# A hybrid attention and convolution backbone on one core: the sink logit as a score column, and rows of h that all start 160 bytes past a multiple of 256

## The reference

```python
h = modulate(rmsnorm(x, g_mix[l]), sh1, sc1)
hc = modulate(rmsnorm(ctx, g_mix[l]), csh1, csc1)
q, k, v, u = split_in(h @ w_in[l])
...
s_loc = jnp.einsum('bnqhgd,bnkhd->bnhgqk', qb, kb).astype(jnp.float32) * SCALE
s_loc = jnp.where(valid[None, :, None, None], s_loc, NEG_INF)
s_ctx = jnp.einsum('bnqhgd,bchd->bnhgqc', qb, k_ctx).astype(jnp.float32) * SCALE
s_sink = jnp.broadcast_to(sink.astype(jnp.float32).reshape(N_KV_HEADS, GROUP, 1, 1), ...)
p = jax.nn.softmax(jnp.concatenate([s_loc, s_ctx, s_sink], axis=-1), axis=-1)
...
x = x + gt1 * merge_groups(a_out, cv_out, g_attn_out[l], g_conv_out[l], w_out[l])
h2 = modulate(rmsnorm(x, g_ffn[l]), sh2, sc2)
x = x + gt2 * swiglu(h2, w_gate_up[l], w_down[l])
```

## Time and profile before

| | us |
|---|---|
| median of 3 runs | 1558.81 (1558.37 to 1560.59) |
| the profiled execution | 1558.88 |
| its span | 1557.1 |
| layer 0: first products of h to the end of attention | 42 to 307 |
| layer 0: output projection and FFN | 308 to 945 |
| layer 1: products of h up to the attention | 945 to 1060 |
| layer 1: attention | 1060 to 1132 |
| layer 1: output projection, FFN, last norm | 1132 to 1557 |

### The profile page before, as it was taken

How to read it: one execution, slowest core, us unless ns; L and a number is a source line. 1 busy time by engine, 2 the same in 40 slices (tenths; PEclk the granted TensorE clock), 3 DMA queues, 4 the chain that set the end, 5 groups by cost and what they waited for, 6 DMA issues and landing times.

```text
span 1557.1 us, 22716 instructions
## 1 busy us (share of the span) xinstructions
PE 1514.7 (97%) x8830; PEld 1227.4 (79%) x8830; DVE 917.5 (59%) x1529; ACT 535.0 (34%) x869; POOL 103.1 (7%) x147
## 2 busy tenths in 40 slices
PE   5999998999999999999999999999999999999997
PEld 2875775588888888888888888776679888888886
DVE  2684679777566425665863366869977533333335
ACT  3311469725322112221112243238835322222232
POOL 0043100040000000000000000530020000000000
PEclk9999999999999999999999999999999999999999
DMA  9582510013333123433431123520012332322222
GB/s 354 222 230 76 205 52 28 1 41 122 108 121 121 54 94 109 148 114 123 168 108 54 57 65 108 142 67 15 28 58 92 95 96 96 104 96 94 95 91 85
DMA packets 39865, 161.16 MB, mean 104 GB/s; under 512 B 5616, under 2 KB 6000, under 8 KB 33648
## 3 DMA queue, kind: packets, MB, share of 16 engines
q1 hardware_dynamic: 35856, 148.72, 27.9%
q0 software_dynamic: 3936, 11.45, 2.7%
HBM read 149.76 MB, written 2.10 MB: 98 GB/s over the span
## 4 chain that ended last, share of the span: by engine, by line
PE 90%; DVE 5%; ACT 2%; issue 2%; DMA 1%; SPq 0%; DVEq 0%; ACTq 0%
PE banks L514 75%; PE banks L543 3%; PE banks L655 2%; PE banks L667 2%; PE banks L682 2%; PE banks L451 2%; PE banks L717 1%; PE banks L483 1%; PE banks L501 1%; ACT prob L882 1%; DVE row_max L1232 1%; ACT probT L894 1%; DMA ada_first<-in_w_ada 1%; DVE ada_sum_context L1199 0%; DVE x L1208 0%
## 5 line engine op out<-in xcount | busy, mean ns | idle before, releaser
L798 ACT ACTIVATE w_high<-raw 128x1024 fp32r<-128x1024 f32 (+2 forms) x182 | 186.2, 1023 | 714.7 <-PE banks L514 701.6
L1113 DVE TENSOR_TENSOR w_low<-raw,w_high 128x1024 fp32r<-128x1024 f32 (+2 forms) x182 | 217.3, 1194 | 228.2 <-ACT w_high L798 224.8
L514 PE MATMUL banks<-h_high,w_high 128*128 128x512 f32 (+1 forms) x1248 | 309.9, 329 | 2.9 <-DVE tmp L1160 1.1
L514 PE MATMUL banks<-h_high,w_low 128*128 128x512 f32 (+1 forms) x1248 | 304.1, 325 | 0.0
L514 PE MATMUL banks<-h_low,w_high 128*128 128x512 f32 (+1 forms) x1248 | 303.2, 324 | 0.0
L514 PEld LDWEIGHTS banks<-h_high,w_high 128*128 128x128 f32 x1248 | 192.7, 188 | 38.0 <-issue 16.9
L514 PEld LDWEIGHTS banks<-h_low,w_high 128*128 128x128 f32 x1248 | 192.9, 188 | 20.9
L514 PEld LDWEIGHTS banks<-h_high,w_low 128*128 128x128 f32 x1248 | 191.5, 188 | 20.5
L1159 DVE COPY shift_product<-banks 128x2 f32<-128x2 f32 x78 | 12.4, 159 | 198.7 <-PE banks L514 188.1
L514 PE MATMUL banks<-h_normal_high,w_high 128*128 128x512 f32 x304 | 118.3, 389 | 0.0
L514 PE MATMUL banks<-h_normal_low,w_high 128*128 128x512 f32 x304 | 118.3, 389 | 0.0
(11 more groups left out here) (195 smaller groups left out, 2173.6 us busy)
## 6 DMA issues: line engine op xcount, KB each, us to landing
raw<-in_w_gu SPq DMA_DIRECT2D x88, 512.0 KB, 3.5
ada_raw<-in_w_ada SPq DMA_DIRECT2D x21, 1024.0 KB, 5.7
raw<-in_w_dn SPq DMA_DIRECT2D x32, 512.0 KB, 3.5
raw<-in_w_mix SPq DMA_DIRECT2D x28, 512.0 KB, 5.0
ada_in_ff<-in_w_ada SPq DMA_DIRECT2D x12, 1024.0 KB, 5.5
raw<-in_w_out SPq DMA_DIRECT2D x16, 512.0 KB, 3.5
ada_first<-in_w_ada SPq DMA_DIRECT2D x7, 1024.0 KB, 14.4
raw<-in_w_dn SPq DMA_DIRECT2D x16, 384.0 KB, 3.0
```

The lines of the kernel that those rows point to most:

```text
L514: last = mm(bank[:, 2 * slot + bk, 0:b - a], weights[w][:, k0_w + k, :], rhs[:, k0_rhs + k, a:b], start=(k == 0 and n == 0), stop=(k == kt ...
L798: last = f(wH[j][:, at, :], raw[j][:, at, :], ACT.Copy)
L1113: last = tt(wL[j][:, at, :], raw[j][:, at, :], f32(wH[j][:, at, :]), ALU.subtract)
```

## The change

- Queries are multiplied by SCALE when they are split into high and low, so the scores come scaled (`q_high`, `q_low`; TENSOR_TENSOR becomes SCALAR_TENSOR_TENSOR there).
- The sinks are split into three bf16 parts once, at the start, in three rows of a zero tensor; `scores` gets one more product, a bf16 tile of ones by a column of that tensor, which writes the sink logit as one more score column.
- `row_max` runs over the scores and that column and writes its result negated; `neg_max` is gone. The exponential covers the column too, so the row sum has the sink in it; `esink` and `add_sink` are gone.
- DVE's order in a step is invert(n+2), divide(n+2), row_max(n+4).
- `h_high` and `h_low` become one tensor with rows of 832 floats (3328 bytes, 13 x 256). The token columns of every row of both start 160 bytes past a multiple of 256, the shift columns for the latents sit directly before them and those for the context directly behind. Where a pass is split 256 and 258, it is now 258 (two shift columns and 256 tokens) and 256.
- The room for software DMA descriptors is 8192 bytes per partition in place of 16384. Every other tensor keeps its place against the 256-byte grid, or is one that the products of L514 don't read.

```diff
-HC = N + 2
-HW = HC + L + 2
+H0 = 64
+HW = H0 + T
+LINE = 8
...
+        sb("gap_line_h", [P, LINE])
-            hH = h_scope.enter_context(nc.sbuf_tensor("h_high", [P, DT, HW], F32R))
-            hL = h_scope.enter_context(nc.sbuf_tensor("h_low", [P, DT, HW], F32R))
+            h_both = h_scope.enter_context(nc.sbuf_tensor("h_both", [P, 2 * DT * HW + H0 + 56], F32R))
+            flatH, flatL = h_both[:, 0:DT * HW + H0], h_both[:, DT * HW:2 * DT * HW + H0]
+            hH, hL = Rows(flatH), Rows(flatL)
...
-            return [(0, 0, N), (1, HC, HW)] if context else [(0, 0, N // 2), (1, N // 2, HC)]
+            if context:
+                return [(0, H0, H0 + N), (1, H0 + N, HW + 2)]
+            return [(0, H0 - 2, H0 + N // 2), (1, H0 + N // 2, H0 + N, 2)]
...
+                    h = g * GRP + i
+                    parts.append((first + P * len(keys), 1, onesb[:], sink_rows[:, layer, h:h + 1]))
...
-                    f(probs[u % 4][:, 0:w], score_place(u, qs[q][2]), ACT.Exp,
-                      bias=nmax[:, c:c + 1], scale=SCALE, accum_out=psums[:, c:c + 1])
-                    f(esink[:, c:c + 1], col("sink", qs[q][0] * GRP + i, layer), ACT.Exp,
-                      bias=nmax[:, c:c + 1]).then_inc(exp_ok, 1)
+                    f(probs[u % 4][:, 0:w + 1], score_place(u, qs[q][2]), ACT.Exp,
+                      bias=nmax[:, c:c + 1], accum_out=psums[:, c:c + 1]).then_inc(exp_ok, 1)
...
-                    nc.vector.reduce_max(mx[:, c:c + 1], score_place(u, qs[q][2]), AX.X).then_inc(row_ok, 1)
...
+                    nc.vector.reduce_max(nmax[:, c:c + 1], score_place(u, qs[q][2]), AX.X, negate=True).then_inc(max_ok, 1)
...
                     if 0 <= n + 2 < len(order):
-                        add_sink(n + 2)
+                        invert(n + 2)
+                        divide(n + 2)
                     if n + 4 < len(order):
                         row_max(n + 4)
-                    if 0 <= n + 2 < len(order):
-                        invert(n + 2)
-                    if n + 4 < len(order):
-                        neg_max(n + 4)
-                    if 0 <= n + 2 < len(order):
-                        divide(n + 2)
...
+            for n in range(3):
+                rest = sink_rest[:] if n else sinks
+                row = slice(32 * n, 32 * n + 1)
+                chain.link(nc.vector.tensor_copy(sink_part[:], rest))
+                made = nc.vector.tensor_copy(sink_rows[row], sink_part[row])
+                if n == 2:
+                    made.then_inc(sinks_ok, 1)
+                else:
+                    chain.link(tt(sink_rest[:], rest, sink_part[:], ALU.subtract))
```

More of the change, by code:

```diff
@@ L113, in queries, with __init__, __getitem__ @@
             for b in range(TB if layer == 0 else NB)]
+class Rows:
+    def __init__(self, flat):
+        self.flat = flat
+    def __getitem__(self, key):
+        _, k, cols = key
+        return self.flat[:, k * HW + cols.start:k * HW + cols.stop]
 class Chain:
@@ L512, in tile_product @@
                     for n, (weights, rhs) in enumerate(((wH, rhsH), (wH, rhsL), (wL, rhsH))):
-                        for bk, a, b in cols:
-                            last = mm(bank[:, 2 * slot + bk, 0:b - a], weights[w][:, k0_w + k, :],
+                        for bk, a, b, *to in cols:
+                            to = to[0] if to else 0
+                            last = mm(bank[:, 2 * slot + bk, to:to + b - a], weights[w][:, k0_w + k, :],
                                       rhs[:, k0_rhs + k, a:b], start=(k == 0 and n == 0),
@@ L636, in scores @@
                         pe.wait_ge(conv_ok, (CT - 1) * (layer + 1))
+                        pe.wait_ge(sinks_ok, 1)
                     if n < 2:
@@ L767, in _ @@
                               (layer, "n2") if c == 0 else None, blocks)
-                    phase(layer, f"dn{c}", tiles, ffH[layer], ffL[layer], tok_cols(context, False),
+                    phase(layer, f"dn{c}", tiles, ffH[layer], ffL[layer], tok_cols(context),
                           (ff_low, layer * FT + sum(CHUNKS[:c])))
@@ L824, in high @@
                 for a, b, scale in scales:
-                    last = f(hH[:, k, hcols(a, b)], src[:, a:b], ACT.Copy, scale=scale)
+                    last = f(tileH[:, k, hcols(a, b)], src[:, a:b], ACT.Copy, scale=scale)
                 last.then_inc(high_ok, 1)
             def shift_high(layer, shift):
-                for at in (N, HW - 2):
-                    last = f(hH[:, :, at:at + 2], mod[:, layer, shift * DT:(shift + 1) * DT, :], ACT.Copy)
+                for to in shiftsH:
+                    last = f(to, mod[:, layer, shift * DT:(shift + 1) * DT, :], ACT.Copy)
                 last.then_inc(sh_high, 1)
@@ L875, in exponential @@
                 def exponential(n):
-                    u, (q, i) = unit0 + n, order[n]
+                    u, (q, _) = unit0 + n, order[n]
                     w, c = P * len(qs[q][2]), u % 4
@@ L1076, in dn_pair @@
                                     for a, b, v in streams(True):
-                                        last = f(hH[:, t, hcols(a, b)], x[:, t, a:b], ACT.Copy,
+                                        last = f(tileH[:, t, hcols(a, b)], x[:, t, a:b], ACT.Copy,
                                                  scale=gain[:, layer + 1, 0, bass.ds(t, 1), v])
@@ L1144, in low @@
                 for a, b, scale in scales:
-                    last = stt(out=hL[:, k, hcols(a, b)], in0=src[:, a:b], scalar=scale,
-                               in1=f32(hH[:, k, hcols(a, b)]), op0=ALU.mult, op1=ALU.subtract)
+                    last = stt(out=tileL[:, k, hcols(a, b)], in0=src[:, a:b], scalar=scale,
+                               in1=f32(tileH[:, k, hcols(a, b)]), op0=ALU.mult, op1=ALU.subtract)
                 last.then_inc(h_ok, 1)
@@ L1150, in shift_low @@
                 dve.wait_ge(sh_high, 2 * layer + (1 if shift == 0 else 2))
-                for at in (N, HW - 2):
-                    last = tt(hL[:, :, at:at + 2], mod[:, layer, shift * DT:(shift + 1) * DT, :],
-                              f32(hH[:, :, at:at + 2]), ALU.subtract)
+                for to, high in zip(shiftsL, shiftsH):
+                    last = tt(to, mod[:, layer, shift * DT:(shift + 1) * DT, :], f32(high), ALU.subtract)
                 last.then_inc(sh_ok, 1)
@@ L1265, in attention @@
                 row_max(0)
-                neg_max(0)
                 rope_product(layer, LAST_Q, context)
```

84 lines of the change are left out of this document (40 added, 44 removed).

## The result

The changed kernel takes 1545.12 us (median of 4 runs, 1544.04 to 1545.38) against 1558.59 us for the kernel before in the same session: a ratio of 0.9911, 95% interval 0.9896 to 0.9925, 13.5 us faster. The prediction said 1553.3 us, 1548.5 to 1559.5. The profiled execution took 1544.04 us with a span of 1542.2.

The account below looks back on a forecast made before the run. PE was taken to bound the kernel, busy 97% of the span and 90% of the chain. Terms -4.5 - 6.3 + 1.3 + 2.9 + 1.0 = -5.6 us from 1558.88 gave 1553.3 us, range 1548.5 to 1559.5.

Parts of the forecast that it names:

- Rows of h: Main products on h in layer 0: 2880 matmuls at 173.95 ns in place of 175.5, 4.5 us gained; layer 1 at 0.
- 0.45 ns a column: Products on h: price per column from a pair of ff, making one more column per matmul 173.5 + 0.45 = 173.95 ns.
- The rival that the placing brings nothing: Products on h: their new starts gain nothing, total gain only 1.1 us, 1557.8 us; chance 0.15.
- The removed instructions: Attention: pieces on the chain of esink (3.8 us), neg_max (2.1) and add_sink (0.4), 6.3 us gained; elsewhere worth nothing.
- The column: Attention on PE: the sink's one-column product costs 0.06 us on 48 units of the chain, 2.9 us (0.5 to 5.8).
- The division behind the inverse: Attention on DVE: division starts 0.20 us after the inverse, 0.13 us back on about ten units, 1.3 us lost.
- What stays: Attention: 1.0 us (0 to 2) of the 6.3 remains because PE's own string or the probabilities' copy is late next.
- Between 236 and 262: Layer 0's attention, where ACT is the chain: units some 2 us shorter in all.
- The column's own rival: Attention on PE: switching weights to the ones and back costs 0.24 us a unit, 11.5 us, giving 1561.9; chance 0.08.
- the late maximum: Attention on DVE: maximum comes too late, 0.4 us in each of 32 units, +12.8 us, giving 1566; chance 0.05.
- More is gained: Whole kernel: column hides at 0.01 us, nothing stays, h reaches ff's pace; -10.3 us, 1548.6; chance 0.12.
- What costs nothing: Query scaling, start-up sink rows, smaller descriptor room (2.1 us slack) and one more column in maximum and exponential: no term.

Follow-up runs that it names:

- rows_32: The changed kernel with all rows of h starting 32 bytes past a multiple of 256 in place of 160; 1554.24 us, ratio 0.9968.
- rows_128: The changed kernel with all rows of h starting 128 bytes past a multiple of 256 in place of 160; 1553.61 us, ratio 0.9966.
- rows_192: The changed kernel with all rows of h starting 192 bytes past a multiple of 256 in place of 160; 1554.89 us, ratio 0.9969.
- rows_only: The kernel before with only the new rows of h and the smaller descriptor room, attention as before; 1553.45 us, ratio 0.9967.
- all_back: The changed kernel with small exponential, sum step and negation put back as idle copies in DVE's old order, sink column kept; 1552.95 us, ratio 0.9964.
- two_columns: The changed kernel with a second one-column product, of zeros, onto the same score column in every unit; 1546.45 us, ratio 0.9921.
- no_column: The changed kernel without the sink's product and its score column, so the softmax leaves out the sink; 1544.13 us, ratio 0.9908.
- max_first: The changed kernel with DVE's order maximum, inverse, division in place of inverse, division, maximum; 1545.60 us, ratio 0.9912.
- att_only: The kernel before with only the change of attention, rows of h and descriptor room as before; 1552.15 us, ratio 0.9956.
- esink_back: The changed kernel with the sink's small exponential on ACT put back behind every exponential, its result unused, only signalling; 1553.02 us, ratio 0.9949.
- add_back: The changed kernel with a small DVE instruction, multiplying the sum by one, put between exponential and inverse; 1548.76 us, ratio 0.9936.
- weights_0: The changed kernel, rows of h at 160, with weight tiles moved from 128 past a multiple of 256 to a multiple; 1562.70 us, ratio 1.0025.

## Why the prediction was wrong

**Rows of h: mechanism right, term too small.** Forecast -4.5 us for 2880 products at 173.95 ns, and 0 for layer 1. Measured 173.4 ns: 2.1 ns less each, 6.0 us by the product, and 6.7 us in all stretches of h together, layer 1's included (its 222 products went from 120.7 to 118.5 ns, where I had counted that one gain and one loss cancel). The step that failed is the added "0.45 ns a column": a pair of h takes the 347 ns of a pair of ff, so the two extra columns are free. The second step is layer 1, put at 0: its stretches gave 1.3 of the 6.7 us. The intervals from start to start show where the gain lies. Before, 231.0 ns follow a product of 512 columns and 119.8 one of 258; after, 230.0 and 116.7. Most came from the context columns, which had started 8 bytes past a multiple of 16. Some of that comes with all the even starts tried: in rows_32, rows_128 and rows_192 the 258 columns take 117.6 to 118.3 ns, while their 512 columns take 235.0 to 235.8. The 512-column products were anything from 226 to 236 ns in the walk of 16 bytes, by row and by which weights they met.

The reason given for ff's pace was wrong as well: I took 160 for a good place of the moving rows. For h it is good at a distance of 32 bytes from the weights; ff kept its pace with the weights moved, which stays unexplained.

**The rival that the placing brings nothing** is refuted by the 2.1 ns and by rows_only alone, 0.9967 with 1 outside its interval. It rested in part on SBUF — State Buffer, section Door 1, in the Trainium skill, with 16-byte lines as the grid of a row. The gain on the context columns agrees with a grid of 16 bytes. The four even starts of h do not: all are multiples of 32 and two paces, 173.4 and 176.7 ns, stand there.

**Attention: the steps that failed.** They are the statement that the removed instructions outside the chain's pieces are worth nothing, and the column's 0.06 us. Forecast: -6.3 for the removed instructions, +1.3 for the division, +2.9 for the column, +1.0 that stays: -1.1 net. Measured: -7.5 in the width.

- *The removed instructions.* Forecast net of division and remainder -4.0; all_back against the changed kernel says -7.0 for the same three edits. I had counted only the pieces that the chain names, and said that elsewhere they "run beside PE and are worth nothing". They were worth something in the dense units, where the scores waited for `esink` inside PE's chain: units 13 to 28 of layer 1 took 32.1 us and take 30.6 by the starts of their turns, units 33 to 44 of layer 0 20.0 and 19.1. That is 2.3 of the 7.5 us, in stretches that I had put at nothing. The gap of 0.05 us between turn and scores stands in the timeline above.
- *The column.* Forecast 2.9 us (0.5 to 5.8); 0.2 in the width, 1.0 by the medians. Scaling the spacing in a stream of fp32 one-column products was wrong for this place: the product stands in the 0.21 us between mask and values that were there before. The second column adds 0.026 us to a unit, still under half of 0.06. In the Trainium skill, TensorE: Matmul & The Clock Gate, section Back-to-back issue gap, gives about 60 cycles, 25 ns, for a product of 1 to 64 columns; from this figure 48 units would be 1.2 us, an estimate. The trace agrees where two such products follow each other: 0.03 us in two_columns, 28 to 42 ns over its 80 units. Between the mask's product and `values` the start stands 0.12 us behind the one and 0.09 ahead of the other, and the medians can't tell 1.2 us from their 1.0.
- *The division behind the inverse*, 0.20 us, was right in the row. *What stays* was right in kind: the first four units of layer 0 lost 1.6 us, and the next four took 0.9 back.
- *Between 236 and 262* I forecast some 2 us, and this was right: the sixteen units there took 29.5 us by first and last turn and take 27.2 (compare the chain of the earlier trace rows):

```profile
L667 PE MATMUL banks<-ident,prob x41: 272/273/329, 234.6 to 264.1; 128*128 128x128 f32 x41
```
```profile
L692 PE MATMUL banks<-ident,prob x41: 272/273/331, 231.9 to 259.1; 128*128 128x128 f32 x41
```

**The other rivals.** The column's own rival (0.24 us each) fell by a unit's 0.006 us and by no_column's 1.0 us in all, the late maximum by 0.99 us of slack and by max_first. "More is gained" came closest in kind: nothing to pay for the column, ff's pace for h. Its 1548.6 stopped at the chain's 6.3 us, and it had 0.12. **What costs nothing** did cost nothing: the small copies at the start and the smaller descriptor room show in no stretch. No run has the descriptor room alone; it is part of rows_only and of the changed kernel.

## What to carry to other kernels

Where PE is the chain, look at the spacing of its matmuls, not at their records: two matmuls 0.57 us apart that are 0.52 us apart elsewhere hide a wait that no chain names, and a small instruction that delays it has a price in every such unit. Remove small dependent instructions together and measure the whole: here one of three, left in the new order, kept 60% or more of the cost. For products of fp32r (the split high and low parts) tune the start of the moving rows against the start of the weights, shape by shape, and look up where each tensor ended up in the layout after each edit: one that is moved for one stretch can cost 5.7 ns a product in another.

## What was not expected of the hardware

The pace of one and the same product, 512 and 258 columns of fp32r, depends on two starts in SBUF together: 173.4 ns at a distance of 32 bytes from weights to rows, with either pair of starts, and 176.7 at 0, 64 and 160 modulo 256. For products of 512 columns alone distance 0 is the fast one (226.7 ns), and both distances tried beside it are slow: 232.4 with the weights at 0, 233.3 with the rows at 160. Why, and why ff does not follow h's rule, stays open.

The granted clock fell for about 10 us at the end of layer 0's attention in some kernels (0.54 in rows_only, 0.53 in att_only and esink_back, 1.00 before and after), which cost 4.7 us in each. Five more profiles, add_back, max_first, rows_128, rows_192 and weights_0, have a shorter fall at the same place (max_first 0.57 over 302 to 306 us); in add_back and max_first the way from the last turn to the first attn product is 43.3 us, 1.5 more than before. PE's busy share ahead of it does not tell it: from 290 to 303 us PE was busy for 12.16 us in esink_back, where the clock fell, and for 12.20 in all_back, where it did not. What tips it was not settled.
